# One-core decoder stack on Trainium2: output-projection chunks placed among the last attention heads, and a re-ordered opening

## The chip, the cores and the metric

The kernel runs on one core of a Trainium2 chip. The metric is the device time in microseconds of one execution. TensorE (PE) does the matrix products, VectorE (DVE) and ScalarE (ACT) the elementwise work, GpSimd (POOL) squares, clears and gathers, SyncE (SP) issues the weight transfers.

## What is computed

The reference is one sequence of 256 tokens, width 1024, through two blocks. Cut to what matters here:

```python
def first_block(x, ...):
    h = x
    for i in range(2):
        h = h + 0.5 * swiglu(rmsnorm(h, ffn_norm_a[i]), ...)      # hidden width 2816
        m = rmsnorm(h, mix_norm[i])
        h = h + (mla_mixer(m, ...) if i == 0 else nsa_mixer(m, ...))
        h = h + 0.5 * swiglu(rmsnorm(h, ffn_norm_b[i]), ...)
    return rmsnorm(h, final_norm)
def mla_mixer(...):   # 16 heads, causal softmax attention
    ...
    return o @ w_o    # (256 x 1024) @ (1024 x 1024)
def nsa_mixer(...):   # 16 heads, selected and window attention, gated
    ...
    return o.reshape(B, S, H * NSA_V) @ w_o
```

The second block (sliding-window and stick-breaking attention, then a layer that gathers 128 expert rows per token block) is not touched.

## The kernel before, in words

Activations are kept transposed: `hT` holds 8 chunks of 128 features by 256 tokens. Every product of weights and activations is done in three passes for precision (`three`, L541 to L543): weight high x activation high, weight high x activation low, weight low x activation high. So one *chunk* of a product is 3 matmuls of 128x256, and one output column block (8 chunks) is 24.

Weights come as *units* of 128x1024 (`plan`). SP moves them in order into `raw`, a ring of 9 slots (L564). ACT copies each into `WH` (the high part, L656, in `hi`), DVE subtracts to get `WL` (the low part, L1016, in `lo`); both rings have 5 slots. `hi` and `lo` run up to 3 units ahead of the one asked for. TensorE frees a slot with the semaphore `s_used`. Activations are split likewise: ACT writes `XH` (`high_x`, L665), DVE writes `XL` (`low_x`, L1024). `X` and `Y` are two such pairs.

Each engine has its own program, written out in order; semaphores join them.

**The opening.** SP loads the first constants (204 columns, with the block of ones), x in two halves, and then the units. ACT makes the eight `XH`, then splits the units `gate` 0, `up` 0, and so on. DVE does the same with the low parts. POOL squares x (`squares(0)`, L588) at the same time as these. TensorE starts the `gate` product when the whole low part of the first unit is there, then does `up`, then the sum of the squares (`sums`, L1648), which the root and reciprocal for the norm wait for.

**Attention.** Head pairs go through a pipeline `attention(...)`: in step i TensorE computes the scores of pair i+1 (L1798, L1928), the values product of pair i-3 (`values`, L1721 and L1722; for every second NSA step also L1955) and the transposes of pair i-2 (`turn`, L1713). ACT takes exponentials (L731), copies the transposes (L724) and writes the high part of the output (L712); DVE adds the bias or mask, takes the maxima (L1117, L1118), scales (L1105) and writes the low part (L1082, semaphore `s_ol`, one count per 128-feature chunk). MLA has 8 pairs and 11 steps, NSA 16 and 19. Scores lie in PSUM banks 0 to 3, transposes in 4 and 5, values in 6 and 7.

**The output projection.** `project` on TensorE comes after the last step:

```python
project("mla_o", (7, 0, 1, 6) * 2, X, (s_ol, O_MLA),
        [(s_ol, O_MLA + 8), None, None, None] + [(s_h, H0[1] + k + 1) for k in range(4)])
```

The first entry makes it wait for all 8 chunks, since bank 7 holds the last pair's values. `project` on DVE adds each column block to `hT` (L1072), splits one more weight unit and writes the low part of the next stage's input; ACT and POOL follow. Then comes the next feed-forward part, whose first `gate` and `up` products (`opening`) take their input chunk by chunk. The three first projection units are split before attention begins.

Of the kernel before, what the change touches and what calls it, by code (L numbers as in the profile page):

```python
# [10 lines left out]
ACT = mybir.ActivationFunctionType  # L11
# [3 lines left out]
T = 256  # L15
# [219 lines left out]
AHEAD = 4  # L235
# [22 lines left out]
def program(nc, wst, cst, x, skt, uv, out, vscr, cscr, units):  # L258
    ctx = ExitStack()
    with ctx:  # L260
# [315 lines left out]
        def pool_program(po):  # L576
            def squares(p):
                for kc in range(8):
                    h_wait(po, p, kc)
                    if p and kc == 0:  # L580
                        po.wait_ge(s_sums, p)
                        if p == 2:
                            po.wait_ge(s_c5s, 2)
                        if p == 6:
                            po.wait_ge(s_xl, 8 * p + 8)
                        if p == 7:
                            po.wait_ge(s_qas, 1)
                    po.tensor_tensor(SQ[:, kc, :], hT[:, kc, :], hT[:, kc, :], ALU.mult).then_inc(s_sq, 1)  # L588
# [54 lines left out]
        def act_program(ac):  # L643
            own = Own(ac, o_act)
            at_m = [0]

            def hi(name, n):

                while at_m[0] < min(U(name, n) + AHEAD - 1, NSPL):
                    m = at_m[0]  # L650
                    i = spl_unit[m]
                    w = units[i][1]
                    ac.wait_ge(s_raw[i % RAW], 16 * (i // RAW + 1))
                    if m >= SPL:
                        ac.wait_ge(s_used, m - SPL + 1)
                    ac.activation(WH[:, m % SPL, 0:w], raw[:, i % RAW, 0:w], ACT.Copy).then_inc(s_hi, 1)  # L656
                    at_m[0] = m + 1
# [9 lines left out]
            def prenorm(p):  # L667
                if p == 6:
                    ac.wait_ge(s_gg, 1)
                for kc in range(8):  # L670
                    high_x(p, kc)
                if p in (1, 3, 4):
                    ac.wait_ge(s_sums, p)
# [66 lines left out]


            ac.wait_ge(s_c[0], 16)
            prenorm(0)
            ffn(0)
            ac.wait_ge(s_c[1], 16)
# [259 lines left out]
        def dve_program(dv):  # L1005
# [122 lines left out]

            dv.wait_ge(s_c[0], 16)
            for kc in range(8):  # L1130
                low_x(0, kc)
            ffn(0)
            dv.wait_ge(s_c[1], 16)
# [83 lines left out]
                return ins  # L1217

            attention(J_MLA, 8, ST, mla_bias, None, lambda j: low_out(XL, XH, j, 6 + j % 2, O_MLA + j))
            project("mla_o", (7, 0, 1, 6) * 2, 2)  # L1220
            dv.wait_ge(s_tbm, 1)
            dv.wait_ge(s_plain, plain_n[where["ohc"][0]])
            dv.tensor_copy(NST[0:16, 0, 0:384], PS[0:16, 7, 0:384])
# [102 lines left out]
            def nsa_low(k):  # L1326
                if k % 2 == 1:
# [1 line left out]

            attention(J_NSA, 16, NST, nsa_bias,  # L1330
                      lambda k: GT[:, :, 2 * (k // 2):2 * (k // 2) + 2, 1 + k % 2].rearrange("p b e -> p e b"), nsa_low)
            project("nsa_o", (7, 0, 1, 6) * 2, 5)
            ffn(3)

            for t in range(5):
# [277 lines left out]
        def pe_program(pe):  # L1613
# [83 lines left out]
                        down(f - 1)  # L1697
                down(NF - 1)

            def project(name, banks, X, x, bank_waits):  # L1700
                for t in range(8):
                    if bank_waits[t]:
                        pe.wait_ge(*bank_waits[t])
                    gemm(name, t, 0, 8, X, PS[:, banks[t], 0:T], x=x if t == 0 else None).then_inc(s_used, 1)

            def turn(J0, k, ST_):
                st = ST_[:, k % 3, :].rearrange("p (e k) -> p e k", e=2)
# [15 lines left out]
                return ins  # L1723

            pe.wait_ge(s_c[0], 16)
            ffn(0)
            pe.wait_ge(s_c[1], 16)

# [74 lines left out]
            for i in range(11):  # L1803
# [12 lines left out]
                if 0 <= i - 2 < 8:  # L1816
                    if i == 2:
                        pe.wait_ge(s_vm, 4)
                    turn(J_MLA, i - 2, ST)
            project("mla_o", (7, 0, 1, 6) * 2, X, (s_ol, O_MLA),  # L1820
                    [(s_ol, O_MLA + 8), None, None, None] + [(s_h, H0[1] + k + 1) for k in range(4)])
            pe.wait_ge(s_h, H0[1] + 5)
            pe.matmul(PS[0:16, 7, 0:384], c("rel")[0:33, :], c("ohx")[0:33, :], start=True, stop=True,
                      skip_group_check=True).then_inc(s_tbm, 1)
            R, s, v = plain("ohc", 0)
# [107 lines left out]
            for i in range(19):  # L1933
# [24 lines left out]
                if 0 <= i - 2 < 16:  # L1958
                    if i == 2:
                        pe.wait_ge(s_vsw, 1)  # L1960
                    turn(J_NSA, i - 2, NST)
            project("nsa_o", (7, 0, 1, 6) * 2, Y, (s_ol, O_NSA),
                    [(s_ol, O_NSA + 8), None, None, None] + [(s_h, H0[4] + k + 1) for k in range(4)])
            ffn(3)

            opening(6, "qa", 0, PS[:, 0, 0:T], "qa", 1, PS[:, 1, 0:T])
# [295 lines left out]
```

## Time and profile before

| what | value |
|---|---|
| median of 3 runs | 1963.95 us (1962.52 to 1964.80) |
| the profiled execution | 1965.77 us, its span 1963.9 us |
| granted TensorE clock, mean of the span | 0.986 of full |
| busy PE, DVE, ACT, POOL | 1792.6, 1290.3, 918.0, 294.6 us |
| weight loads of TensorE | 1431.2 us |
| moved | 485.02 MB |

Busy time is summed by engine over the span. A matmul's duration is modelled and runs into the next one's, so the distance between two starts is what one costs. The chain of waits follows the work that ended last back from step to step; idle time before an instruction is put down to what released it. The clock column gives the share of full speed that was granted.

### The profile page before, as it was taken

The numbers are of one execution on the slowest core, as the hardware profiler recorded it, in microseconds if no ns is written. First come the engines' busy times: TensorE is split into PE (matmuls) and PEld (weight loads), VectorE is DVE, ScalarE is ACT, GpSimd is POOL, SyncE is SP. The second block draws the span as 40 slices with busy tenths as digits, with TensorE's granted clock in tenths as the row PEclk, the third lists the DMA queues.
The fourth block names the chain that finished last, engine by engine and source line by source line (L and its number), as shares of the span: only waits on it lengthen the run. The fifth ranks groups of instructions, "written<-read, shape, count | busy, mean of one in ns | idle before, by whom it ended". The sixth has DMA issues, their size and how long they took to land.

```text
span 1963.9 us, 29274 instructions
## 1 busy us (share of the span) xinstructions
PE 1792.6 (91%) x11274; PEld 1431.2 (73%) x11274; DVE 1290.3 (66%) x2375; ACT 918.0 (47%) x1896; POOL 294.6 (15%) x323
## 2 busy tenths in 40 slices
PE   6999999999999999999999788999987877788777
PEld 6999988999999999789999678986433322223222
DVE  5655885665666565976556766868677776776444
ACT  4444554444544453754445436634544444344343
POOL 2000001000000000010001000223433333333331
PEclk9999999999999999999999889999999999999999
DMA  7556434975455545135555333579999999999998
GB/s 269 182 189 193 128 104 128 242 264 184 156 202 181 181 144 178 58 100 169 183 193 161 119 108 108 173 255 389 405 421 421 421 422 421 421 422 421 421 421 320
DMA packets 96138, 485.02 MB, mean 247 GB/s; under 512 B 10576, under 2 KB 10832, under 8 KB 62976
## 3 DMA queue, kind: packets, MB, share of 16 engines
q0 software_dynamic: 38544, 275.25, 36.3%
q1 hardware_dynamic: 57456, 207.90, 31.7%
q8 instruction: 90, 1.47, 0.3%
q14 instruction: 48, 0.39, 0.1%
HBM read 478.65 MB, written 4.46 MB: 246 GB/s over the span
## 4 chain that ended last, share of the span: by engine, by line
PE 61%; DMA 13%; DVE 10%; issue 8%; POOL 4%; ACT 3%; another core or an unknown queue 0%; POOLq 0%; SPq 0%; ACTq 0%; DVEq 0%
PE PS L541 17%; PE PS L542 16%; PE PS L543 16%; DMA WH<-uv,A 3%; PE PS L2153 3%; DMA YL<-uv,A 3%; DMA A<-uv,A 2%; DMA raw<-uv,A 2%; PE PS L2174 2%; PE PS L1648 1%; DVE WL L1016 1%; POOL raw L639 1%; DMA WL<-uv,A 1%; DMA XF<-uv,A 1%; DMA YH<-uv,A 1%
## 5 line engine op out<-in xcount | busy, mean ns | idle before, releaser
L1016 DVE TENSOR_TENSOR WL<-raw,WH 128x1024 fp32r<-128x1024 f32 (+1 forms) x375 | 447.7, 1235 | 85.9 <-ACT WH L656 85.5
L541 PE MATMUL PS<-XH,WH 128*128 128x256 f32 x1616 | 463.6, 287 | 26.4 <-DVE WL L1016 15.8
L542 PE MATMUL PS<-XL,WH 128*128 128x256 f32 x1616 | 458.9, 284 | 0.0
L543 PE MATMUL PS<-XH,WL 128*128 128x256 f32 x1616 | 458.6, 284 | 0.0
L656 ACT ACTIVATE WH<-raw 128x1024 fp32r<-128x1024 f32 (+1 forms) x375 | 371.3, 1042 | 37.6 <-PE PS L543 17.0
L541 PEld LDWEIGHTS PS<-XH,WH 128*128 128x128 f32 x1616 | 309.3, 191 | 31.1 <-issue 19.7
L542 PEld LDWEIGHTS PS<-XL,WH 128*128 128x128 f32 x1616 | 309.6, 192 | 0.2
L543 PEld LDWEIGHTS PS<-XH,WL 128*128 128x128 f32 x1616 | 309.2, 191 | 0.0
L959 ACT ACTIVATE A<-A,RTK 128x1 f32<-128x1 f32 x256 | 75.2, 294 | 297.3 <-DVE A L1604 295.8
L541 PE MATMUL PS<-GH,WH 128*128 128x256 f32 x704 | 198.1, 281 | 0.0
L542 PE MATMUL PS<-GL,WH 128*128 128x256 f32 x704 | 197.8, 281 | 0.0
L543 PE MATMUL PS<-GH,WL 128*128 128x256 f32 x704 | 197.8, 281 | 0.0
L701 ACT ACTIVATE A<-A 128x256 f32<-128x256 f32 x88 | 36.8, 419 | 341.1 <-DVE A L1045 341.1
L541 PE MATMUL PS<-YH,WH 128*128 128x256 f32 x584 | 165.2, 283 | 3.2 <-DVE WL L1016 1.5
L542 PE MATMUL PS<-YL,WH 128*128 128x256 f32 x584 | 164.1, 281 | 0.0
L543 PE MATMUL PS<-YH,WL 128*128 128x256 f32 x584 | 164.0, 281 | 0.0
L1045 DVE TENSOR_TENSOR A<-PS,RT 128x512 f32<-128x512 f32 x88 | 60.9, 692 | 141.4 <-PE PS L543 141.0
L2153 PE MATMUL PS<-raw,A 128*128 128x512 f32 x260 | 126.9, 613 | 28.7 <-ACT A L967 28.7
L541 PEld LDWEIGHTS PS<-GH,WH 128*128 128x128 f32 x704 | 132.6, 188 | 0.1
L542 PEld LDWEIGHTS PS<-GL,WH 128*128 128x128 f32 x704 | 132.7, 188 | 0.0
L543 PEld LDWEIGHTS PS<-GH,WL 128*128 128x128 f32 x704 | 132.7, 188 | 0.0
L2153 PEld LDWEIGHTS PS<-raw,A 128*128 128x128 f32 x260 | 45.7, 191 | 106.9 <-issue 106.9
(306 smaller groups left out, 2985.9 us busy)
## 6 DMA issues: line engine op xcount, KB each, us to landing
raw<-wst SPq DMA_DIRECT2D x381, 512.0 KB, 4.6
raw<-wst SPq DMA_DIRECT2D x8, 384.0 KB, 3.1
vscr<-A POOLq DMA_DIRECT2D x1, 3072.0 KB, 37.0
A<-vscr POOLq DMA_DIRECT2D x1, 2048.0 KB, 22.3
C<-cst SPq DMA_DIRECT2D x1, 1236.5 KB, 11.3
raw<-uv,A POOLq DMA_INDIRECT x65
hT<-xin SPq DMA_DIRECT2D x2, 512.0 KB, 5.8
A<-vscr POOLq DMA_DIRECT2D x1, 1024.0 KB, 11.9
```

Of the source, the lines that this page charges most:

```text
L541: pe.matmul(o, wh, xh, start=start, stop=False, skip_group_check=True)
L542: pe.matmul(o, wh, xl, start=False, stop=False, skip_group_check=True)
L543: return pe.matmul(o, wl, xh, start=False, stop=stop, skip_group_check=True)
L639: po.indirect_dma_start(row, None, uv if row.dtype == F32 else uv.bitcast(F32R), bass.IndirectOffsetOnAxis(ap=EX[:, blk, s:s + 1].bitcast( ...
L656: ac.activation(WH[:, m % SPL, 0:w], raw[:, i % RAW, 0:w], ACT.Copy).then_inc(s_hi, 1)
L701: ac.activation(GS[:, b, 0, :], GS[:, b, 0, :], ACT.Silu).then_inc(s_silu, 1)
L959: own(ac.activation(AG[:, blk, s:s + 1], AV[:, blk, s:s + 1], ACT.Gelu, scale=RTK[:, blk:blk + 1]))
L1016: dv.tensor_tensor(WL[:, m % SPL, 0:w], raw[:, i % RAW, 0:w], f32(WH[:, m % SPL, 0:w]), ALU.subtract).then_inc(s_lo, 1)
L1045: dv.tensor_tensor(GS[:, b], PS[:, b, :].rearrange("p (a t) -> p a t", a=2), RT[:, 1:2, :].broadcast_to([128, 2, T]), ALU.mult).then_inc(s ...
L1648: ins = pe.matmul(PS[:, 7, 0:T], c("ones"), SQ[:, kc, :], start=kc == 0, stop=kc == 7, skip_group_check=True)
L2153: ins = pe.matmul(PS[:, YB[blk] + q, :], DG[:, g % 4, :], v[:, 512 * q:512 * q + 512], start=False, stop=s == 127, skip_group_check=True)
L2174: ins = pe.matmul(PS[:, bank_q[n], 0:T], R[:, 128 * kc:128 * kc + 128], XF[:, kc, :], start=kc == 0, stop=kc == 7, skip_group_check=True)
```

## The change

Five edits. (1) TensorE does nine products of ones with the first constants, into a PSUM bank that is written over later, before it waits for anything but the constants. (2) ACT does a one-column copy before it waits for x; the table load goes ahead of that copy. (3) ACT and DVE split the first weight unit between x's fourth and fifth chunk. (4) POOL's squares of x wait for the last low part of x. (5) In both attentions, chunks of the first three column blocks of the output projection go into the last steps, into banks 0, 1 and 2 (`part`); `project` does what is left of them, each one's last chunk last, then blocks 3 to 7. MLA places 3, 4 and 5 chunks, NSA 5, 5 and 5.

```diff
@@ POOL: squares
                     h_wait(po, p, kc)
+                    if p == 0 and kc == 0:
+                        po.wait_ge(s_xl, 8)
@@ ACT: prenorm, and the start
                 for kc in range(8):
+                    if p == 0 and kc == 4:
+                        hi("gate", 0, 0)
                     high_x(p, kc)
...
             ac.wait_ge(s_c[0], 16)
+            ac.activation(small[:, 63:64], c("eps", 0, 1), ACT.Copy)
             prenorm(0)
@@ DVE
             for kc in range(8):
+                if kc == 4:
+                    lo("gate", 0, 0)
                 low_x(0, kc)
...
-            project("mla_o", (7, 0, 1, 6) * 2, 2)
+            project("mla_o", (0, 1, 2, 3) * 2, 2)
...
-            project("nsa_o", (7, 0, 1, 6) * 2, 5)
+            project("nsa_o", (0, 1, 2, 3) * 2, 5)
@@ TensorE
-            def project(name, banks, X, x, bank_waits):
-                for t in range(8):
-                    if bank_waits[t]:
-                        pe.wait_ge(*bank_waits[t])
-                    gemm(name, t, 0, 8, X, PS[:, banks[t], 0:T], x=x if t == 0 else None).then_inc(s_used, 1)
+            def part(name, t, X, k0, k1, O0):
+
+                H, L = weights(name, t)
+                for kc in range(k0, k1):
+                    pe.wait_ge(s_ol, O0 + kc + 1)
+                    w = slice(128 * kc, 128 * kc + 128)
+                    ins = three(pe, PS[:, t % 4, 0:T], H[:, w], L[:, w], X[0][:, kc, :], X[1][:, kc, :], kc == 0, kc == 7)
+                return ins
+
+            def project(name, X, O0, h0, begun):
+
+                for t in range(3):
+                    part(name, t, X, begun[t], 7, O0)
+                for t in range(3):
+                    part(name, t, X, 7, 8, O0).then_inc(s_used, 1)
+                for t in range(3, 8):
+                    if t >= 4:
+                        pe.wait_ge(s_h, h0 + t - 3)
+                    gemm(name, t, 0, 8, X, PS[:, t % 4, 0:T]).then_inc(s_used, 1)
...
             pe.wait_ge(s_c[0], 16)
+
+            for n in range(9):
+                pe.matmul(PS[:, 6, 0:c_cut], c("ones"), C[:, 0:c_cut], start=True, stop=True, skip_group_check=True)
             ffn(0)
@@ TensorE, MLA steps
+                if 7 <= i < 10:
+                    pe.wait_ge(s_bias, J_MLA + (8 if i == 9 else 7))
+                    part("mla_o", i - 7, X, 0, i - 4, O_MLA)
-            project("mla_o", (7, 0, 1, 6) * 2, X, (s_ol, O_MLA),
-                    [(s_ol, O_MLA + 8), None, None, None] + [(s_h, H0[1] + k + 1) for k in range(4)])
-            pe.wait_ge(s_h, H0[1] + 5)
+            project("mla_o", X, O_MLA, H0[1], (3, 4, 5))
@@ TensorE, NSA steps
+                if 15 <= i < 18:
+                    pe.wait_ge(s_bias, J_NSA + (16 if i == 17 else 15))
+                    part("nsa_o", i - 15, Y, 0, 5, O_NSA)
-            project("nsa_o", (7, 0, 1, 6) * 2, Y, (s_ol, O_NSA),
-                    [(s_ol, O_NSA + 8), None, None, None] + [(s_h, H0[4] + k + 1) for k in range(4)])
+            project("nsa_o", Y, O_NSA, H0[4], (5, 5, 5))
```

How the order changes on the engines, first on ACT at the very start. Before:

```order
L665 ACT_TABLE_LOAD [waits x0]
L665 ACTIVATE XH<-hT,C 128x256 [waits consts0]
L665 ACTIVATE XH<-hT,C 128x256 x3
L665 ACTIVATE XH<-hT,C 128x256 [waits x1]
L665 ACTIVATE XH<-hT,C 128x256 x3
L656 ACTIVATE WH<-raw 128x1024 [waits raw_landed0]
```

And with the change:

```order
L747 ACT_TABLE_LOAD
L747 ACTIVATE small<-C 128x1 [waits consts0]
L667 ACTIVATE XH<-hT,C 128x256 [waits x0]
L667 ACTIVATE XH<-hT,C 128x256 x3
L658 ACTIVATE WH<-raw 128x1024 [waits raw_landed0]
L667 ACTIVATE XH<-hT,C 128x256 [waits x1]
L667 ACTIVATE XH<-hT,C 128x256 x3
```

The table load no longer waits for x, and the first unit's high part stands between the two halves of x.

Second, TensorE at the end of the NSA steps (the products of L1721, in the change L1742, are the values of a head, those of L1713, in the change L1734, its transposes). Before, from the transposes of the last pair on:

```order
L1713 MATMUL PS<-C,A 128x128 [waits p_copied,p_scaled]
L1713 MATMUL PS<-C,A 128x128 x2
L1713 MATMUL PS<-C,A 128x128 [waits p_copied]
L1713 MATMUL PS<-C,A 128x128 x2
L1721 MATMUL PS<-A 64x256 [waits p_copied]
L1722 MATMUL PS<-A 64x128
L1721 MATMUL PS<-A 64x256 [waits p_copied]
L1722 MATMUL PS<-A 64x128
L1955 MATMUL PS<-XF,A 64x256 [waits cmp_p_copied,vc_tokens]
L1955 MATMUL PS<-XF,A 64x256
L541 MATMUL PS<-YH,WH 128x256 [waits o_low,weight_low]
```

With the change the same place, to the first of the chunks that now stand before the values:

```order
L1734 MATMUL PS<-C,A 128x128 [waits p_copied,p_scaled]
L1734 MATMUL PS<-C,A 128x128 x2
L1734 MATMUL PS<-C,A 128x128 [waits p_copied]
L1734 MATMUL PS<-C,A 128x128 x2
L541 MATMUL PS<-YH,WH 128x256 [waits o_low,weight_low,scores_read]
L542 MATMUL PS<-YL,WH 128x256
L543 MATMUL PS<-YH,WL 128x256
L541 MATMUL PS<-YH,WH 128x256 [waits o_low]
L542 MATMUL PS<-YL,WH 128x256
L543 MATMUL PS<-YH,WL 128x256
```

Fifteen such products follow these transposes, and only then the last pair's values. The two steps before have fifteen each as well.

## Rows read from the trace of the kernel before

**Rows 1.** The page: what the DMA engines moved, by 40th of the span.
```profile
GB/s 269 182 189 193 128 104 128 242 264 184 156 202 181 181 144 178 58 100 169 183 193 161 119 108 108 173 255 389 405 421 421 421 422 421 421 422 421 421 421 320
```
**Rows 2.** The chain that ended last, first 15 us: start us, us, what.
```profile
6.65 1.28 ACT L665
7.95 0.52 ACT XH L665
8.58 4.94 DVE XL L1024 x8
13.53 1.15 DVE WL L1016
14.76 0.55 PE PS L541
```
**Rows 3.** The timeline of the opening: start us, us, engine, line, operation.
```profile
0.75 0.39 SPq L547 DMA_DIRECT2D C<-cst  x1
2.13 2.51 SPq L564 DMA_DIRECT2D raw<-wst  x4
6.72 5.34 POOL L588 TENSOR_TENSOR A<-hT 128x256 f32<-128x256 f32 x8 [6.26 <-DMA hT<-xin]
11.15 3.89 ACT L656 ACTIVATE WH<-raw 128x1024 fp32r<-128x1024 f32 x4
22.93 3.61 PE L1648 MATMUL PS<-A,C 128*128 128x256 f32 x16
```
**Rows 4.** DMA issues of the first 2.4 us: size, median us to landing.
```profile
raw<-wst SPq DMA_DIRECT2D x1, 512.0 KB, 7.0
C<-cst SPq DMA_DIRECT2D x1, 102.0 KB, 2.0
```
**Rows 5.** The low part of an activation chunk, ns min/median/max: opening, then MLA's projection.
```profile
L1024 DVE SCALAR_TENSOR_TENSOR XL<-hT,C,XH x8: 474/786/832, 8.6 to 13.1; 128x256 fp32r<-128x256 f32 x8
...
L1024 DVE SCALAR_TENSOR_TENSOR YL<-hT,C,YH x8: 474/477/484, 310.7 to 328.4; 128x256 fp32r<-128x256 f32 x8
```
**Rows 6.** Windows: stretch, its length, busy (instructions), last columns clock, DMA share, GB/s.
```profile
14.76:20.02 5.26, 5.26 (x24) 1.00 1.03 411
296.20:304.40 8.20, 5.29 (x38) 1.00 0.01 2
844.70:853.80 9.10, 6.71 (x47) 1.00 0.01 2
1090.00:1210.00 120.00, 101.19 (x682) 0.87 0.37 119
```
**Rows 7.** TensorE's timeline: the first product after three idle gaps.
```profile
1086.87 0.39 PE L541 MATMUL PS<-XH,WH 128*128 128x256 f32 x1 [2.81 <-DVE RT L1341]
1127.96 0.58 PE L541 MATMUL PS<-XH,WH 128*128 128x256 f32 x1 [2.55 <-DVE A L1401]
1146.84 0.58 PE L541 MATMUL PS<-XH,WH 128*128 128x256 f32 x1 [1.84 <-DVE A L1401]
```
**Rows 8.** TensorE's timeline at MLA's last steps and the first projection product.
```profile
297.16 0.72 PE L1721 MATMUL PS<-A 128*64 128x256 f32 x3 [0.81 <-ACT A L724]
298.70 0.87 PE L1713 MATMUL PS<-C,A 128*128 128x128 f32 x6 [0.38 <-DVE A L1105]
304.43 0.39 PE L541 MATMUL PS<-XH,WH 128*128 128x256 f32 x1 [0.93 <-DVE XL L1082]
```
**Rows 9.** The same at NSA's last steps.
```profile
852.20 0.65 PE L1955 MATMUL PS<-XF,A 15*64 15x256 f32 x4
853.79 0.39 PE L541 MATMUL PS<-YH,WH 128*128 128x256 f32 x1 [0.94 <-DVE YL L1082]
```
**Rows 10.** DVE's timeline in MLA's projection: one column block and the next.
```profile
313.25 0.42 DVE L1072 TENSOR_TENSOR hT<-PS,hT 128x256 f32<-128x256 f32 x1 [0.89 <-PE PS L543]
313.59 0.48 DVE L1024 SCALAR_TENSOR_TENSOR YL<-hT,C,YH 128x256 fp32r<-128x256 f32 x1
313.98 1.22 DVE L1016 TENSOR_TENSOR WL<-raw,WH 128x1024 fp32r<-128x1024 f32 x1
316.09 0.42 DVE L1072 TENSOR_TENSOR hT<-PS,hT 128x256 f32<-128x256 f32 x1 [0.88 <-PE PS L543]
```
**Rows 11.** DVE and POOL in NSA's projection.
```profile
854.26 1.23 DVE L1016 TENSOR_TENSOR WL<-raw,WH 128x1024 fp32r<-128x1024 f32 x1 [0.52 <-ACT WH L656]
...
863.35 1.64 DVE L1016 TENSOR_TENSOR WL<-raw,WH 128x1024 fp32r<-128x1024 f32 x1
...
863.12 0.79 POOL L588 TENSOR_TENSOR A<-hT 128x256 f32<-128x256 f32 x1 [2.06 <-DVE hT L1072]
```

More of the change, by code:

```diff
@@ L645, in act_program, with hi @@
             at_m = [0]
-            def hi(name, n):
-                while at_m[0] < min(U(name, n) + AHEAD - 1, NSPL):
+            def hi(name, n, past=AHEAD - 1):
+                while at_m[0] < min(U(name, n) + past, NSPL):
                     m = at_m[0]
```

## The prediction

> **What bounds the kernel now.** I read the chain of waits first: where its steps are TensorE products back to back, only fewer or earlier products help; where it runs through other engines, their order is what counts. In the first 15 us it is not TensorE: the chain goes from x's landing through ACT's table load (1.28), one high part, DVE's eight low parts (4.94) and the first weight unit's low part (1.15) to TensorE's start at 14.76 [rows 2]. From there TensorE is nearly always busy, so whatever starts it earlier shifts what follows. I looked next at its timeline at the ends of the two attentions. In MLA from 296.2 to 304.4 it is busy 5.29 of 8.20 us, in NSA from 844.7 to 853.8 busy 6.71 of 9.10 [rows 6]; each stretch starts after the transposes of the pair two before the last and ends where the projection has got the last low part [rows 8, 9]. Last the transfers: from about 1325 us on the DMA engines move 421 GB/s without a break [rows 1]. That late phase is bound by its gathers, but its first gather needs the results of all that stands before it, so a shift passes through it.
>
> **The unit prices.** A product of 128x256 costs 2.84 us / 24 = 0.118 us at full clock: two additions to hT lie 2.84 apart, with 24 products between [rows 10]. After the start 24 products take 5.26 us, 0.219 each [rows 6]: that spacing is the 1.2 GHz level, 0.118 the 2.4 GHz one, although the clock column shows 1.00 for both. A first product after a gap shows which level holds by its own duration, 0.39 or 0.58 [rows 7].
>
> **Term 1: TensorE starts earlier.** The table load loses its wait for x, so it falls into time in which ACT has nothing to do, and the first high part can begin at 6.65 instead of 7.95 [rows 2]. Eight high parts ran before the units began, from 7.95 to 11.15 [rows 2, 3], 0.40 each, so four are done at about 8.3. The first unit was issued at 2.13 and landed 7.0 later, at 9.1 [rows 3, 4]. So ACT waits 0.8 us for it; this is late next. Its high part takes a quarter of 3.89, 0.97 [rows 3], to 10.1; its low part 1.15 [rows 2] with a handover of 0.1 to 11.4; TensorE starts at 11.5. Gain 14.76 - 11.5 = **3.2 us**. Chunks 5 to 8 of x then come at about 0.4 each from 11.4 on (0.477 long without POOL beside it [rows 5], 0.39 from start to start [rows 10]), ready at 13.0. TensorE needs the fifth only after 12 products, at 12.9 or later. The low part of `up` is done at 14.3, where TensorE needs it after 24 products, at 14.3 at the earliest.
>
> **Term 2: the nine idle products.** They need only the constants, issued at 0.75 and landed 2.0 later [rows 3, 4], so they start near 2.8. A sum over 256 columns takes 3.61/8 = 0.45 at full clock [rows 3]; 204 columns at half that clock take 0.72, nine 6.5, or less if the clock rises among them. They end by about 9.3, before 11.5, so they delay nothing. What they may bring is 24 products at 0.118 in place of 0.219: at most 2.4 us; at the least nothing, since a gap of over 2 us follows. Of three gaps of that size in this trace, one (2.81) was followed by the full clock, two (2.55 and 1.84) by the lower one [rows 7]. I take the lower one as likelier, and **0.5 us** for a slow stretch that may be shorter than that of before. The ends stay for the range. The Trainium skill (TensorE: Matmul & The Clock Gate, "What's actually happening") says that the number of slow products at a start varies from run to run; one trace can't show that.
>
> **Term 3: POOL's squares move behind x.** They took 5.34 [rows 3], and now run from 13.0 to about 18.5. TensorE wants them after 48 products, at 17.2 at the earliest, and the last of the eight 3.1 later, at 20.3. Cost 0; without this cover of 1.8 us a late square would delay root, reciprocal and all behind.
>
> **Term 4: MLA's last steps.** Moved are 12 chunks, 36 products, 4.25 us; with what `project` now does of blocks 0 to 2 before the last chunk is needed (9 chunks, 3.2 us), 7.4 us of work may go ahead of the last low part. The room is smaller: idle 8.20 - 5.29 = 2.9 us, plus five products ahead of gaps whose modelled durations (0.28, against a spacing of 0.118) count 0.16 too long, 3.7 in all. The first filler (9 products, 1.06) fits into the idle 0.81 and pushes the values by about 0.1. The idle 0.38 before the transposes [rows 8] comes before any filler of its step and stays. The later fillers (1.4 and 1.8 us) are longer than their gaps, so the last values product is late by some 2 us; but then 9 chunks of the same three blocks stand ready to hide the last pair's copies. So TensorE is its own bound and gains what idle it fills: 3.7 - 0.4 = **3.3 us**. DVE must keep up: 0.34 + 0.39 + 1.22 = 1.95 per column block, 15.6 for eight [rows 10], against 14.2 for five blocks of TensorE plus the 5 us in which the next `gate` and `up` go through chunks 1 to 7. Nothing behind waits more. SP's queue and the weight ring are not bound here: the three units were split before.
>
> **Term 5: NSA's last steps.** Idle 9.10 - 6.71 = 2.4, plus six ends of 0.16: 3.35. Fillers of 15 products (1.77) are longer than every gap and start in front of the first, so all of it is filled: **3.3 us**. The unit for block 3 is late next: its low part ends 2.6 us after the last values product (852.85 to 855.49 [rows 9, 11]); TensorE has 27 products, 3.2 us, until it needs it. DVE with POOL beside it takes 0.34 + 0.39 + 1.64 = 2.37 per block [rows 10, 11], 19.0 for eight; TensorE needs its last low part 0.7 + 14.2 + 5.0 = 19.9 after the first block is free. It holds, by 0.9.
>
> **The sum.** 3.2 + 0.5 + 0 + 3.3 + 3.3 = 10.3 us. The profiled execution took 1965.77 for a span of 1963.9, which is 1.8 above the median of the runs; its sum is 1955.5, and the median's is 1963.95 - 10.3 = **1953.7 us**.
>
> **A rule against it.** Where POOL squares beside DVE, DVE's low part of a unit takes 1.64 in place of 1.22, and the square 0.79 [rows 10, 11]: 0.42 lost, about half a square. The Trainium skill (SBUF — State Buffer, "Who interferes with whom") says more: a DVE instruction with two SBUF inputs and a GpSimd one that reads SBUF exclude each other for the whole instruction. The trace agrees on the conflict, not on its full length. What it would do is rival C.
>
> **Rivals.**
> - **A, the full clock from the start.** The idle products keep the clock up to 11.5, and all 24 products gain: 2.4 in place of 0.5. 1951.8 us. For it: the gap of 2.81 [rows 7]; against: the other two.
> - **B, the fillers push the heads.** Each delayed values product delays its copy, and through it the next transposes, so that half the filled idle opens again further on: 3.3 of 6.6. 1957.0 us. Against it: the last transposes depend on DVE's scaling, which was ready before.
> - **C, whole-instruction exclusion.** A block in NSA's projection then takes 0.34 + 0.39 + 1.22 + 0.79 = 2.74, eight 21.9, 2.0 past TensorE's need; and in the opening four low parts and squares alternate, four squares follow: 13.0 + 4 x 1.84 + 4 x 0.62 = 22.8, about 0.8 late. Gain 7.5, 1956.4 us.
> - **D, slower: the clock further on.** Between 1090 and 1210 us the granted clock is 0.87 [rows 6], up to 15.6 us of full clock lost, from gaps such as those of rows 7. If the shift lets the gaps fall so that twice as much is lost, 15.6 is added: 1969.3 us. It decides from 1.7 times on. Against it: the three runs lie within 2.3 us.
> - **E, one part does not do what it says**, for instance fillers that wait on a weight unit and fill nothing: 7 us less, 1960.7.
>
> **How the numbers follow.** A difference of 0.2% (3.9 us) is what a measurement can tell from none. The forecast has 0.57 with its own spread of 1.5 us each way, A 0.17, B 0.11, C 0.07, E 0.05, D 0.03. The range from 1950.0 to 1957.6 holds the forecast, A, B and C, with their unknowns somewhat over 8 in 10. Faster than 1960.0: 0.92; within: 0.05; slower: 0.03.
>
> **What would show it.** First product of L541 at 11.5, before it nine products ending by 9.3; table load before 3 us; its first 24 products take 2.8 (A) or up to 5.3. No idle before MLA's and NSA's projection above 0.4; the distance from the last values product to the last column block 3.3 shorter than the products' number would give. Wrong would be: an idle before block 3 for a WL, before the sums for a square, or at chunk 8 of the next opening for DVE.

## The result, and the profile after

| | before | changed |
|---|---|---|
| median of the runs, same chip (us) | 1964.38 (1962.52 to 1965.49, 4 runs) | 1952.33 (1951.70 to 1953.21, 4 runs) |
| ratio, 95% interval | | 0.9942 [0.9928, 0.9956] |
| profiled execution, its span | 1965.77, 1963.9 | 1953.21, 1951.4 |

The gain is 12.05 us, between 8.6 and 14.1 by the interval. 10.3 were forecast, so the prediction was right, and the measurement cannot tell its size from the forecast. A second set of runs of both kernels, below, has 10.99. The time by itself therefore proves little about the terms. The traces do, if they are cut at the same instructions. The marks are: **x**, where x has landed (the start of ACT's first high part; before, the start of the table load, which held the wait for x); **P**, the first L541 product; **S**, the start of the sums of squares on TensorE; **R**, the reciprocal of the first root; **M** and **N**, the last addition of a column block to hT in MLA's and NSA's projection; **G**, the first gather; **E**, the end of the span.

| us | x to P | P to S | S to R | x to R | R to M | M to N | N to G | G to E |
|---|---|---|---|---|---|---|---|---|
| before | 8.11 | 8.17 | 4.16 | 20.44 | 300.35 | 549.37 | 423.65 | 663.44 |
| changed | 4.94 | 5.78 | 5.91 | 16.63 | 296.74 | 545.81 | 424.01 | 662.45 |
| shorter by | 3.17 | 2.39 | -1.75 | 3.81 | 3.61 | 3.56 | -0.36 | 0.99 |

With x landing 0.89 earlier in this execution the row adds up to the 12.5 us by which the spans differ. The stages that the change touches give 3.8 + 3.6 + 3.6 = 11.0; the other 1.5 lie where nothing was changed. Of the 3.8, part belongs to this one profile of before: its P to S, 8.17, holds a longer stretch at the 1.2 GHz level than another profile of the same opening has (7.37, first batch).

The chain of waits of the changed kernel, first 22 us (start us, us, what), to be laid beside [rows 2]:

```profile
2.13 6.18 DMA raw<-wst
8.33 1.06 ACT WH L658
9.42 1.22 DVE WL L1021
10.64 1.59 DVE XL L1029 x4
12.40 6.98 POOL A L590 x5
19.43 2.41 PE PS L1655 x8
```

The head of the chain is now the first weight unit's transfer, as forecast ("this is late next"). But TensorE does not take the chain over at its first product, as it did at 14.76. The chain goes on through DVE and **POOL's squares**, to which the prediction gave a cost of 0. The timeline of the opening shows how (start us, us, engine, line, operation, count, then idle time before and its releaser):

```profile
0.75 1.28 ACT L747 ACT_TABLE_LOAD   x1 [0.75 <-PEq L2281]
2.89 6.23 PE L1749 MATMUL PS<-C 128*128 128x204 f32 x18 [2.89 <-DMA C<-cst]
5.76 1.70 ACT L667 ACTIVATE XH<-hT,C 128x256 fp32r<-128x256 f32 x4 [2.69 <-DMA hT<-xin]
10.70 0.39 PE L541 MATMUL PS<-XH,WH 128*128 128x256 f32 x1 [1.58 <-DVE WL L1021]
12.15 3.49 DVE L1021 TENSOR_TENSOR WL<-raw,WH 128x1024 fp32r<-128x1024 f32 x3
12.40 8.69 POOL L590 TENSOR_TENSOR A<-hT 128x256 f32<-128x256 f32 x8 [11.95 <-DVE XL L1029]
16.48 2.10 PE L1655 MATMUL PS<-A,C 128*128 128x256 f32 x8
17.55 1.35 DVE L1021 TENSOR_TENSOR WL<-raw,WH 128x1024 fp32r<-128x1024 f32 x1 [1.92 <-ACT WH L658]
19.43 2.41 PE L1655 MATMUL PS<-A,C 128*128 128x256 f32 x8 [0.85 <-POOL A L590]
22.39 1.75 DVE L1034 RECIPROCAL RT<-RT 128x256 f32<-128x256 f32 x1 [3.48 <-ACT RT L695]
```

The table load is over before x lands. The nine idle products (18 passes in the records) end at 9.12, and 1.58 us of idle follow. The eight squares take 8.69 us instead of 5.34 [rows 3], and TensorE, through with its 48 products at 16.48, has to wait among the sums. The same squares one by one (ns min/median/max, first and last start; the second and third line are single ones):

```profile
L590 POOL TENSOR_TENSOR A<-hT x8: 603/608/3706, 12.4 to 20.5; 128x256 f32<-128x256 f32 x8
...
L590 POOL TENSOR_TENSOR A<-hT x1: 3706/3706/3706, 12.4 to 12.4; 128x256 f32<-128x256 f32 x1
...
L590 POOL TENSOR_TENSOR A<-hT x1: 1587/1587/1587, 17.8 to 17.8; 128x256 f32<-128x256 f32 x1
```

Six squares take about 0.60. The first takes 3.71: it begins 0.25 after DVE's three low parts of weight units, which run back to back from 12.15 to 15.64, and ends only behind them. The other, 1.59, lies beside DVE's fourth low part at 17.55. The three low parts lose nothing themselves (3.49 / 3 = 1.16 each).

The windows of the changed kernel (stretch, length, busy and instructions of PE, PEld, DVE, ACT, POOL, then clock, DMA share, GB/s) over the 48 first products, the last steps of the two attentions, and the late stretch of rival D:

```profile
10.70:16.48 5.78, 5.78 (x49) 5.78 (x50) 4.94 (x7) 3.14 (x5) 4.08 (x2) 1.00 1.01 418
...
291.40:301.30 9.90, 9.52 (x82) 8.26 (x81) 4.77 (x16) 6.14 (x21) 0.00 (x0) 1.00 0.01 2
836.30:848.00 11.70, 11.70 (x99) 9.61 (x98) 4.51 (x17) 5.78 (x17) 0.00 (x0) 1.00 0.01 1
...
1080.00:1200.00 120.00, 102.44 (x690) 93.05 (x689) 81.48 (x134) 50.65 (x89) 0.00 (x0) 0.87 0.37 120
```

MLA's end is idle for 0.38 us, NSA's for none, where [rows 6] had 2.9 and 2.4. From 294.5 to 345 us and from 836 to 890 us TensorE is busy without a gap: neither a weight's low part before block 3 nor DVE in the next opening holds it, which were two of the prediction's three signs of being wrong. The third, a wait for a square, did occur (0.85, above). The clock further on is 0.87, as it was.

### The profile page after: what moved, and what is told of

Its sections match the earlier page's. It is cut to its first block, busy times and chain, and to the rows that moved or that the text cites. A ratio compares the mean times of both kernels' runs of the same rounds, so it can differ in the third digit from the quotient of the medians.

```text
span 1951.4 us, 29326 instructions
## 1 busy us (share of the span) xinstructions
PE 1793.9 (92%) x11292; PEld 1432.7 (73%) x11292; DVE 1288.2 (66%) x2375; ACT 917.3 (47%) x1897; POOL 297.5 (15%) x323
## 4 chain that ended last, share of the span: by engine, by line
PE 62%; DMA 13%; issue 9%; DVE 8%; POOL 5%; ACT 3%; POOLq 0%; SPq 0%; ACTq 0%; DVEq 0%
PE PS L541 16%; PE PS L542 16%; PE PS L543 16%; PE PS L2180 4%; DMA raw<-uv,A 3%; DMA WH<-uv,A 2%; PE PS L2201 2%; DMA YH<-uv,A 2%; DMA XF<-uv,A 2%; DMA WL<-uv,A 2%; DVE WL L1021 2%; PE PS L1655 1%; POOL raw L641 1%; DMA XH<-uv,A 1%; DMA YL<-uv,A 1%
## 5 line engine op out<-in xcount | busy, mean ns | idle before, releaser
L541 PE MATMUL PS<-XH,WH 128*128 128x256 f32 x1616 | 462.8, 286 | 12.2 <-DVE A L1408 4.4
L541 PEld LDWEIGHTS PS<-XH,WH 128*128 128x128 f32 x1616 | 308.4, 191 | 17.2 <-DVE A L1408 5.7
L541 PE MATMUL PS<-GH,WH 128*128 128x256 f32 x704 | 198.1, 281 | 0.0
L541 PE MATMUL PS<-YH,WH 128*128 128x256 f32 x584 | 165.5, 283 | 2.2 <-DVE WL L1021 1.5
L541 PEld LDWEIGHTS PS<-GH,WH 128*128 128x128 f32 x704 | 132.6, 188 | 0.1
```

The costliest lines, as they stand in the source:

```text
L541: pe.matmul(o, wh, xh, start=start, stop=False, skip_group_check=True)
```

## The experiments

In a run's table the time of before is that of the same chip. The executions of one kernel spread over 1.5 to 6.6 us, so a part worth 1 us is judged by the stages of the profiles, and the times are given beside them.

### First batch: each half alone, the idle products, the wait of the squares

**The opening alone**: before, with the four edits of the opening (idle products, early table load, unit split among x's chunks, POOL's wait for x).

> The kernel before with the four edits of the opening alone. Theory: the opening and the two attention ends each shift the rest and add up; in the trace of the changed kernel the product after the first sums comes 4.7 us earlier (26.19 to 21.49), so 1964.4 - 4.7 = 1959.7 us. Rival: part of the opening's gain is given back before the first attention, or what is gained in sum comes from the late phase: then 1961 or more, or under 1958.5.

**The last heads alone**: the change without those four.

> The kernel before with the chunks among the last heads of both attentions alone. Theory: 3.6 us in MLA and 3.5 in NSA by the additions to hT, so 7.1 less, 1957.3 us. Rival (the fillers push the heads, B of the prediction): 3.3 less, 1961.1 us.

**No idle products**: the change with this taken out.

```
-            for n in range(9):
-                pe.matmul(PS[:, 6, 0:c_cut], c("ones"), C[:, 0:c_cut], ...)
```

> The changed kernel without the nine idle products. Theory: they are what holds the full clock at 10.7; without them the first 24 products take about 5.2 instead of 2.8 us, but the sums waited for POOL's squares, so only about 0.7 us is lost at the first root: 1953.0 us. Rival: the whole 2.4 us is lost, 1954.7 us. Rival 2: the clock would be up anyhow, and nothing changes.

**Squares early**: the change with POOL free to begin its squares as x lands.

```
-                    if p == 0 and kc == 0:
-                        po.wait_ge(s_xl, 8)
```

> The changed kernel without POOL's wait for the last low part of x: the squares start with x again. Theory: the eight squares cost 1.09 each beside the four unit splits (8.69 in sum) and hold the sums up by 1.65 us; early they are hidden, the first root comes about 1.2 us sooner though the unit's low part takes up to 0.4 longer: 1951.1 us. Rival: beside the squares each low part of x takes 0.83 again and TensorE starts 1 us or more later, so that the wait pays: 1953 us or more.

| | median (us) | ratio to before (1965.94) | x to P | P to S | x to R | R to M | M to N |
|---|---|---|---|---|---|---|---|
| opening alone | 1962.78 | 0.9986 [0.9977, 0.9995] | 4.96 | 7.30 | 16.65 | 300.29 | 549.33 |
| last heads alone | 1958.22 | 0.9965 [0.9952, 0.9979] | 8.10 | 7.37 | 19.64 | 296.78 | 547.33 |
| no idle products | 1955.03 | 0.9946 [0.9932, 0.9959] | 4.96 | 7.32 | 16.61 | 296.75 | 544.30 |
| squares early | 1955.90 | 0.9949 [0.9936, 0.9963] | 5.45 | 7.30 | 16.91 | 296.75 | 545.84 |

The halves add up: 3.2 and 7.7 us by the times, 10.9 together, against 12.05 and 10.99 of the whole change in its two sets of runs. For the last heads that is near the 7.1 expected. For the opening 4.7 was expected and 3.2 came: 0.89 of the 4.7 was x landing earlier in one execution, not the change. The last heads alone have before's opening and show x to R at 19.64, not 20.44. So the opening is worth 3.0 to 3.8 at R, by which of the two profiles it is held against. The halves also stay where they are made. With the opening alone R to M and M to N are those of before to within 0.1; with the last heads alone x to P is that of before, and R to M is 3.6 shorter. No idle opens again further on in place of one that was filled, which was rival B.

Without the idle products x to R is 16.61, with them 16.63. Their first product and their sums, from TensorE's timeline of the kernel without them:

```profile
11.40 0.55 PE L541 MATMUL PS<-XH,WH 128*128 128x256 f32 x1 [11.40 <-DVE WL L1021]
...
18.72 3.79 PE L1655 MATMUL PS<-A,C 128*128 128x256 f32 x16
```

The sums follow each other to 22.51 and R stands at 23.05. The changed kernel's TensorE was done with the 48 products 1.54 us sooner after its start (5.78 against 7.32), and got nothing for it, because the last square ended 15.3 us after x in both. So in the kernel as changed the idle products bring nothing to the root, and POOL hides what they bring. The expectation had 0.7 lost at the root and 1953.0 us in all. Nothing was lost there, and the time fits that: 10.9 below its before, as the repeat of the change is by 10.99.

With the squares early they disturb DVE's low parts of x instead:

```profile
6.60 3.20 DVE L1027 SCALAR_TENSOR_TENSOR XL<-hT,C,XH 128x256 fp32r<-128x256 f32 x4 [6.60 <-ACT XH L665]
9.72 1.63 DVE L1019 TENSOR_TENSOR WL<-raw,WH 128x1024 fp32r<-128x1024 f32 x1
```

Four low parts take 3.20, where they take 1.59 to 1.67 without POOL; the unit's low part takes 1.63 instead of 1.22. P comes 0.5 later, R 0.28 later. A gain of 1.2 at the root was expected and did not come; the rival's time did (1953 or more), though TensorE started 0.5 later and not 1. In this run the clock fell among the 48 products (7.30). Had it held, R would stand 1.52 earlier, at 15.4, which is an estimate and ahead of the change; no run shows it. Whether POOL's wait pays when the clock holds is therefore open.

### Second batch: are the squares what holds R?

If POOL's blocked squares set R, moving them to an engine that does not meet DVE must bring R forward, and most so when the clock holds.

**Squares on ACT**: POOL's squares of the first norm are taken out, and ACT does them after the first high part of `gate`:

```
+                        for kc in range(8):
+                            ac.activation(SQ[:, kc, :], hT[:, kc, :], ACT.Square).then_inc(s_sq, 1)
```

> The changed kernel with the eight squares of the first norm on ACT, after it has split the fourth unit, instead of on POOL. Theory: the squares, 1.09 us each on POOL beside DVE's unit splits, hold the first root back; the reciprocal of the first root began 16.6 us after x's first high part in three runs, whatever the clock did. On ACT they take 0.4 each in a stretch in which it idles, so the reciprocal comes 15.0 us after it if the clock is full, 16.5 if it falls; 0.1 to 1.6 us off the whole. Rival: ACT then reaches the fifth unit late and TensorE waits for it at the first down product.

**The same without the idle products.**

> The last one without the nine idle products. Theory: with the squares out of the way the products' worth is seen whole: 48 products take 7.3 us as in three traces with a start at the lower clock, against 5.8 in the trace of the change and 7.3 in two others of kernels with the idle products; so this lies 0 to 1.5 us above the kernel with them. Rival: the idle products give back their full 2.4 us each time.

**Two squares early**: POOL waits for four low parts of x for its first two squares, and for all eight for the rest.

```
-                    if p == 0 and kc == 0:
-                        po.wait_ge(s_xl, 8)
+                    if p == 0 and kc in (0, 2):
+                        po.wait_ge(s_xl, 4 if kc == 0 else 8)
```

> The changed kernel with POOL's first two squares released at the fourth low part of x and the other six at the eighth. Theory: two squares fit into the 1.35 us in which DVE waits for the first unit's high part, and six remain: they end 2.2 us sooner, so that TensorE's sums are no longer held; reciprocal 15.0 to 16.9 us after the first high part. Rival: the two run into the first unit's low part (1.63 instead of 1.22 in the kernel with all squares early) and TensorE starts 0.4 later.

**No unit split**: the change with the first unit behind all eight chunks of x again, on ACT and DVE.

```
-                    if p == 0 and kc == 4:
-                        hi("gate", 0, 0)
...
-                if kc == 4:
-                    lo("gate", 0, 0)
```

> The changed kernel with the first unit split after all eight chunks of x. Theory: the unit lands 2.6 us after x, so ACT would reach it only 0.7 us later than it can begin: TensorE starts 0.6 later, but the squares begin 2.9 sooner and the sums are not held; reciprocal 15.7 us after x's first high part at full clock, 17.3 at the lower. So the placing of the unit is worth about nothing in the end. Rival: it is worth what it moves the start by, 0.6 us or more of the whole.

| | median (us) | ratio to before (1965.38) | x to P | P to S | x to R |
|---|---|---|---|---|---|
| squares on ACT | 1951.41 | 0.9931 [0.9917, 0.9944] | 4.94 | 7.30 | 16.41 |
| the same, no idle products | 1955.78 | 0.9951 [0.9937, 0.9965] | 4.98 | 7.14 | 16.28 |
| two squares early | 1952.82 | 0.9937 [0.9924, 0.9951] | 5.02 | 5.79 | 15.56 |
| no unit split | 1955.77 | 0.9944 [0.9930, 0.9957] | 5.82 | 7.29 | 17.27 |

Two squares done before the run of low parts take most of the wait off the sums when the clock holds: x to R falls from 16.63 to 15.56 at the same P to S. The blocked square is still there, and S to R is 4.75, where sums that wait for nothing have 4.16:

```profile
16.33 2.75 PE L1655 MATMUL PS<-A,C 128*128 128x256 f32 x12
19.27 1.27 PE L1655 MATMUL PS<-A,C 128*128 128x256 f32 x4 [0.19 <-POOL A L590]
...
L590 POOL TENSOR_TENSOR A<-hT x2: 606/608/611, 8.0 to 8.6; 128x256 f32<-128x256 f32 x2
...
L590 POOL TENSOR_TENSOR A<-hT x1: 3797/3797/3797, 12.2 to 12.2; 128x256 f32<-128x256 f32 x1
```

On ACT the eight squares take 0.402 each and the sums run without a gap:

```profile
L702 ACT ACTIVATE A<-hT x8: 402/402/403, 13.7 to 15.8; 128x256 f32<-128x256 f32 x8
...
17.94 3.62 PE L1658 MATMUL PS<-A,C 128*128 128x256 f32 x16
```

But there the clock fell among the 48 products, and then R moves only 0.2 (16.41 against 16.63): with the lower clock TensorE needs the squares about when POOL has them.

Taking the idle products out of that kernel as well was expected to cost 0 to 1.5 us. Its median is 4.4 above, although x to R is 0.13 shorter. The profiled execution is its fastest (1952.02, the other four 1953.63 to 1956.25), so no trace shows what the others lost. This miss stays open, and with it what the idle products are worth in the time.

Without the split P comes 0.88 later, and R 0.63 later than in the repeat of the change below, in which the clock fell too. The theory had it worth nothing in the end; the rival, 0.6 or more, came true. Its rows also show what else was in the 3.17 by which x to P fell:

```profile
5.72 3.30 ACT L667 ACTIVATE XH<-hT,C 128x256 fp32r<-128x256 f32 x8 [2.66 <-DMA hT<-xin]
6.36 3.26 DVE L1027 SCALAR_TENSOR_TENSOR XL<-hT,C,XH 128x256 fp32r<-128x256 f32 x8 [6.36 <-ACT XH L667]
10.00 6.14 DVE L1019 TENSOR_TENSOR WL<-raw,WH 128x1024 fp32r<-128x1024 f32 x4 [0.38 <-ACT WH L658]
...
L590 POOL TENSOR_TENSOR A<-hT x8: 608/1590/1591, 9.8 to 17.7; 128x256 f32<-128x256 f32 x8
```

Here x to P is 5.82, 2.3 below before. The table load gives 1.3 of that. The other 1.0 comes from POOL's wait, edit 4: DVE's eight low parts of x, with no square beside them, take 3.26 in place of 4.94 [rows 2], less 0.4 of waiting for ACT and 0.3 by which the unit's low part is longer. So the 3.17 is some 1.3 for the load, 0.9 for the split and 1.0 for keeping POOL off DVE (with the split in place, squares early cost 0.5).

The squares behave otherwise here than in the change. POOL's first one was under way when DVE's four low parts of units began, and then they took turns: four squares of 1.59 and low parts of 1.49 and 1.63, 6.14 for the four. No square was held for more than one low part.

### Third batch: the change again, more idle products, the fillers taken out

**The change again**, to see whether its 5.78 repeats, **the squares on ACT again**, and **the squares on ACT with twelve idle products** in place of nine (`range(12)`).

> The changed kernel as it is, beside the next three on one chip. Theory: 12 us below the kernel before, as in the first runs; a second profile shows whether its clock is full through the first 48 products (5.8 us) or falls among them (7.3), as in four of six traces with the nine idle products. Rival: always full in this kernel.

> The changed kernel with the first squares on ACT, again, beside the change. Theory: 0.2 us below the change where the clock falls in both, 1.6 where it is full; 0 to 2 us in the median. Rival: no difference or slower.

> The last one with twelve idle products in place of nine, which leave a gap of at most 1.5 us before the first real product in place of 1.6 to 3.7. Theory: with so little idle the clock no longer falls among the first products: 48 of them in 5.8 us, the reciprocal 14.9 us after x's first high part in place of 16.4; 0.5 to 1.5 us off the median. Rival: the gap is not what lets it fall, 48 products still take 7.3, or the idle products end after 10.7 and hold the real ones up by up to 0.6.

**Only the order of the projections**: the change with both `part(...)` blocks of the last steps taken out, and `project` told that nothing was done ahead.

```
-                    part("mla_o", i - 7, X, 0, i - 4, O_MLA)
...
-                    part("nsa_o", i - 15, Y, 0, 5, O_NSA)
...
-            project("mla_o", X, O_MLA, H0[1], (3, 4, 5))
+            project("mla_o", X, O_MLA, H0[1], (0, 0, 0))
```

> The changed kernel with no chunk among the heads, only with the last chunks of blocks 0 to 2 put behind the 21 others. Theory: only the last gap, 0.93 + 0.16, is filled in each attention, so from the first root to MLA's last addition it takes 2.5 us more than with the fillers (299.2 in place of 296.7), and NSA the same: 5 us above the change. Rival: the order within the projection does most of it, 2 us or less above the change.

| | median (us) | ratio to before (1963.01) | P to S | x to R | R to M | M to N |
|---|---|---|---|---|---|---|
| the change again | 1952.02 | 0.9941 [0.9928, 0.9955] | 7.30 | 16.64 | 296.76 | 545.81 |
| squares on ACT again | 1950.39 | 0.9931 [0.9918, 0.9945] | 8.50 | 17.61 | 296.76 | 544.06 |
| ACT, twelve idle products | 1949.98 | 0.9933 [0.9919, 0.9946] | 5.78 | 15.01 | 296.72 | 544.05 |
| only the order | 1953.72 | 0.9953 [0.9939, 0.9967] | 7.31 | 16.63 | 299.33 | 548.59 |

**The clock.** The change again has the same code and another P to S:

```profile
2.85 4.89 PE L1749 MATMUL PS<-C 128*128 128x204 f32 x18 [2.85 <-DMA C<-cst]
11.37 0.39 PE L541 MATMUL PS<-XH,WH 128*128 128x256 f32 x1 [3.63 <-DVE WL L1021]
...
11.37:18.67 7.30, 7.30 (x49) 7.30 (x50) 5.37 (x8) 4.64 (x6) 5.60 (x5) 0.77 1.01 410
...
23.06 1.75 DVE L1034 RECIPROCAL RT<-RT 128x256 f32<-128x256 f32 x1 [3.48 <-ACT RT L695]
```

Its first product takes 0.39, the 2.4 GHz level after 3.63 us of idle, and yet the granted clock of the stretch is 0.77: some products into the work it fell to 1.2 GHz (a spacing of 0.21) for 16 products and rose again. Of nine profiles with nine idle products the clock held through all 48 products in two (5.78, 5.79), fell on the way in five (about 7.30), and was low from the first product or the second in two (7.31, 8.50): 7.1 on average. Four profiles without them, one of them before, show 8.17, 7.37, 7.32 and 7.14: 7.5 on average. So nine are worth 0.4 on P to S, by few profiles that scatter more than that. The two in which it held had 1.58 and 2.75 us of idle ahead of P, but 1.82 and 2.20 also lost it, so the gap alone does not decide. With twelve the clock held, once in one profile:

```profile
2.88 6.91 PE L1752 MATMUL PS<-C 128*128 128x204 f32 x24 [2.88 <-DMA C<-cst]
10.54 0.39 PE L541 MATMUL PS<-XH,WH 128*128 128x256 f32 x1 [0.75 <-DVE WL L1024]
...
16.32 3.61 PE L1658 MATMUL PS<-A,C 128*128 128x256 f32 x16
20.48 1.75 DVE L1037 RECIPROCAL RT<-RT 128x256 f32<-128x256 f32 x1 [1.90 <-ACT RT L694]
```

Here both halves work together: R stands 15.01 behind x, where 14.9 were expected, 1.6 ahead of the change's. This is what a clock that holds can bring once POOL's squares no longer hide it. That twelve make it hold is not shown by one profile: with nine it held in two of nine. The median is 2.0 us below the change's on the same chip, that of the squares on ACT with nine 1.6 below, so twelve against nine is 0.4, where 0.5 to 1.5 was expected. Both intervals overlap the change's. The stages do not make the nine better either: the repeat of the squares on ACT, with the clock low from its first product, has R 0.97 behind the change's.

**The fillers.** Without `part` 1.0 us of MLA's 3.6 and 0.8 of NSA's 3.6 are left. That is what `project` gains by doing the first chunks of its first blocks before any last chunk. DVE then waits 5.42 us for the first block, since three blocks come out together, and 0.89 for the last:

```profile
307.19 0.42 DVE L1077 TENSOR_TENSOR hT<-PS,hT 128x256 f32<-128x256 f32 x1 [5.42 <-PE PS L543]
...
322.10 0.42 DVE L1077 TENSOR_TENSOR hT<-PS,hT 128x256 f32<-128x256 f32 x1 [0.89 <-PE PS L543]
```

The remaining 2.6 and 2.8 come from the fillers in the steps, 5.4 together, where 5 were expected. The median is only 1.7 above the change's, over runs from 1951.88 to 1958.51, which by itself would fit the rival; the profiled execution is the slowest. By the stages the theory holds.

**Why M to N scatters.** Over the kernels with the fillers M to N lies between 544.05 and 547.33, and R to M within 0.06. The windows from 750 to 780 us show why, in the order no idle products, the change, the last heads alone (the granted clock is the third number from the end):

```profile
750.00:780.00 30.00, 30.00 (x222) 28.21 (x221) 20.82 (x32) 13.03 (x15) 0.00 (x0) 1.00 0.46 150
...
750.00:780.00 30.00, 30.00 (x213) 28.35 (x212) 19.39 (x30) 13.03 (x15) 0.00 (x0) 0.94 0.44 139
...
750.00:780.00 30.00, 30.00 (x231) 29.02 (x230) 17.25 (x30) 11.97 (x14) 0.00 (x0) 0.89 0.42 136
```

Where the clock is 1.00 there, M to N is 544.05 to 544.30 (four profiles); at 0.94 it is 545.65 to 545.84 (five profiles); at 0.89 it is 547.1 to 547.3 (two). Before, the opening alone and only the order have 0.94 as well, so their 549.37, 549.33 and 548.59 are rightly held against the change's 545.81. N to G goes the same way: from 1080 to 1200 us the clock is 0.92 and 0.91 in the two profiles with 418.6 and 419.7, and 0.87 to 0.89 in the others (422.6 to 424.2).

## Why the prediction was right, step by step

**Term 1, 3.2 us: right.** x to P is 3.17 shorter in the changed kernel and 3.16 in its repeat. P itself came at 10.70 and not at 11.5, since x and the first unit landed 0.9 and 0.8 earlier in that execution; in the repeat P came at 11.37. ACT waited 0.86 for the first unit, as the term said. Some 1.0 of the 3.17 is owed to edit 4, which keeps POOL off DVE's low parts of x; the term assumed that without naming it.

**Term 2, 0.5 us: near the mean, but nothing of it arrived.** The clock's part is 0.4 by the mean of nine profiles against four. The prediction took "the lower one as likelier" right at P; in fact the clock was high at P in seven of nine profiles and in five of these was lost later, a course that none of its three gaps [rows 7] shows. And what the clock gives ended in the wait for the squares: 16.63 with, 16.61 without. Rival A got its 2.39 us in the profiled execution (P to S) and gave 1.75 back.

**Term 3, cost 0: the step that failed.** It put the squares from 13.0 to about 18.5, with 1.8 us of cover. They ran from 12.40 to 21.09. The first took 3.71, another 1.59. When the clock holds this costs 1.6 us, of which two squares early win back 1.07, and ACT's squares (with twelve idle products) 1.62; when it falls, about 0.2. The price, 5.34 for eight, was that of squares beside low parts of x [rows 3]. The only row beside a unit's low part, 0.79 [rows 11], is of a square that began before it, and met one such instruction and not a run of them.

**The rule against it, rival C.** The prediction read in its row that square and low part conflict, but not for their full length. That reading was wrong. In NSA's projection of the changed kernel:

```profile
861.11 1.63 DVE L1021 TENSOR_TENSOR WL<-raw,WH 128x1024 fp32r<-128x1024 f32 x1
862.66 0.41 DVE L1077 TENSOR_TENSOR hT<-PS,hT 128x256 f32<-128x256 f32 x1
...
864.94 0.41 DVE L1077 TENSOR_TENSOR hT<-PS,hT 128x256 f32<-128x256 f32 x1
...
860.87 0.79 POOL L590 TENSOR_TENSOR A<-hT 128x256 f32<-128x256 f32 x1 [1.50 <-DVE hT L1077]
```

The low part ends 1.08 after the square has ended, and so does every low part of a unit that a square lengthened, in all fourteen profiles (1.08 to 1.09). Every square that a low part lengthened ends 0.47 to 0.48 after that low part, whether it took 0.79, 1.59 or 3.71 (16.11 against 15.64). So the two took their turns in full; the 0.42 of [rows 11] was the rest of a square that had begun first. The Trainium skill (SBUF — State Buffer, "Who interferes with whom") calls the shared port pair "an exclusive lock"; these rows agree. What rival C had wrong in NSA was the price, the square's whole 0.79 per block: blocks follow each other every 2.28 us, as the 2.37 of term 5 had it, not 2.74. In the opening it was nearer than term 3, but for another reason than the alternation it described: one long wait over three low parts and one short one, 8.69 us for the eight, against its 9.8 and the 5.5 of term 3. The alternation itself is what the kernel without the split shows.

**Terms 4 and 5, 3.3 us each: right, 0.3 too small.** R to M is 3.6 shorter in every run with the fillers, M to N 3.5 to 3.7 in every one with before's granted clock of 0.94 between 750 and 780 us. The idle left is the 0.38 before the transposes, as forecast:

```profile
293.96 0.87 PE L1734 MATMUL PS<-C,A 128*128 128x128 f32 x6 [0.38 <-DVE A L1110]
...
299.56 0.66 PE L1742 MATMUL PS<-A 128*64 128x256 f32 x4
300.37 0.39 PE L541 MATMUL PS<-XH,WH 128*128 128x256 f32 x1
```

Rival B's price was 3.3 of 6.6 and is refuted by the first batch. Where the other 0.3 in each attention comes from no run shows.

**The sum.** By the stages 3.8 + 3.6 + 3.6 = 11.0, or 3.0 + 3.6 + 3.6 = 10.2 if the opening is held against the other profile that has before's; the forecast was 10.3. The last heads bring 0.6 more, the opening between 0.7 less and 0.1 more. That it came so near in the profiled execution is luck: the clock gave 2.39 where 0.5 was forecast, and the squares took 1.75 where 0 was. The rest of 12.5 is x's landing and the stretches behind. N to G lies between 418.6 and 424.2 over these kernels and follows the granted clock, as shown above; G to E lies between 661.7 and 666.4, for which no run here shows a cause. The opening alone shows how large that is: its root came 3.8 us earlier relative to x and G to E took 666.4 against 663.44 of before, so its profiled span is only 1.3 below. Rival D asked for a clock well below 0.87 between 1080 and 1200; it is 0.87 in the change. Its mechanism exists, though: the same stretch moved by 5 us the other way in the kernel with the last heads alone.

## What to carry to other kernels

An edit whose cost is hidden needs its price taken in the company that it will have: the squares cost 5.34 beside DVE's low parts of x, 8.69 when they began just behind the start of a run of three low parts of units, and 9.52 when they began just before a run of four. And a gain that ends in a wait shows in no time: x to R was 16.6 with and without the idle products while the squares were on POOL. Off POOL it followed the clock: 15.0 where it held, 16.3 to 17.6 where it did not. Where single executions scatter by several us, cut each profile at the same instructions and add the stages. Before you compare a stage, look at the granted clock in it, in the kernel before too: 0.8 us of this opening's gain, and nearly all of the 3 us of scatter in M to N, lay there.

## What the runs showed of the hardware that was not expected

- DVE's low parts and POOL's squares exclude each other in full: the second of a pair ends a fixed time after the first, 0.47 us for a square and 1.08 for a unit's low part. A square that begins just behind the start of a run of three low parts (3.49) waits for the whole run: 3.70 to 3.80 us in six profiles, for one that takes 0.60 alone. Where a square was under way before the run began, they alternate: four squares of 1.59 in the kernel without the split. What makes DVE keep its turn in the one case and yield it in the other stays open.
- TensorE's granted clock can be at 2.4 GHz for the first products after idle time and fall to 1.2 GHz while they run without a gap: 0.77 over 7.30 us in the change's repeat, 1.00 over 5.78 us in the same code. What decides between them stays open.
- A table load carries the wait of the activation behind it. Given an activation that needs only a constant, it ran at 0.75 instead of 6.65 us.
